# Forgetting attention with scores computed once by rows and probabilities transposed on TensorE, and a bias table stored from another queue

## The chip, the cores and the metric

The kernel runs on one core of a Trainium2 chip. The metric is device time in microseconds of one execution; the figure for the kernel before is the median of 3 runs. Engines: TensorE (PE in the rows; PEld is its weight load), VectorE (DVE), ScalarE (ACT), GpSimd (POOL) and SyncE (SP, whose queue is SPq).

## The reference, cut to what matters

One block of a hybrid encoder over 2048 tokens and 16 meta tokens, width 1024: input LayerNorm, one projection, two groups of 8 attention heads of size 64, output projection, mixture of experts. The change is in the second head group, forgetting attention, and in the store of a small table in the projection.

```python
def forgetting_attention(q, k, v, log_f, key_valid):
    ...
    cum = jnp.swapaxes(jnp.cumsum(log_f, axis=1), 1, 2)
    idx = jnp.arange(lp)
    for i in range(lp // Q_BLOCK):
        lo, hi = i * Q_BLOCK, (i + 1) * Q_BLOCK
        s = jnp.einsum('bqhd,bkhd->bhqk', q[:, lo:hi], k[:, :hi]).astype(jnp.float32) * (HEAD_DIM ** -0.5)
        s = s + cum[:, :, lo:hi, None] - cum[:, :, None, :hi]
        mask = (idx[None, :hi] <= idx[lo:hi, None]) & key_valid[None, :hi]
        p = jax.nn.softmax(jnp.where(mask, s, -jnp.inf), axis=-1)
        outs.append(jnp.einsum('bhqk,bkhd->bqhd', p.astype(v.dtype), v[:, :hi]))
```

The term of the query in `cum` drops out of the softmax; what is added to a score is the negated cumulative sum of its key (`ncum`).

## The kernel before, in words

Stages run one after another with a barrier between: projection (`phase_project`), window attention (`phase_window`), forgetting attention (`phase_forget`), output projection, routing, experts, combination. Everything is fp32. Where a product is to be exact, an operand x is split: ScalarE rounds it to a high part of type fp32r, VectorE computes the low part x - high, and the product is made of two or three fp32r matmuls.

**Forgetting attention** has 8 heads. A unit is one head and a group g = 0 to 3 of 512 queries (4 tiles j of 128), so 32 units. Keys are counted with the 16 meta keys first.

*Rows.* For each query tile (128 queries on partitions) the scores against all its keys are computed in chunks of up to 512 keys (`scores`, L1525): 5, 9, 13 and 17 chunks for the four groups, 44 a head, with 17,664 columns in all. Each chunk takes two matmuls (L1538, L1539), and the diagonal one a third that adds the mask (L1542). VectorE adds `ncum` and takes the maximum in one pass, writing in place in the PSUM bank (`maxima`, L1449, L1459); only the maximum is used. There are three such banks. `tops` (L1463) reduces them to the four negated maxima, splits these, and TensorE turns them to a row (`turn_tops`, L1546), which ScalarE copies into the extra partitions of `q_low` (`copy_tops`, L1383).

*Blocks.* The scores are computed a second time, transposed: for 128 keys on partitions against the unit's 512 queries (`block_scores`, L1554), 44 blocks and 17,664 columns a head, with two matmuls each (L1562, L1565; the second adds the turned maxima) and a mask (L1569). ScalarE takes the exponential twice from PSUM, once to fp32 (`p`, L1395) and once to fp32r (`p_hi`, L1396); VectorE makes `p_lo` (L1479). Four blocks later (`LAG`) `values` (L1573) multiplies by the values with three matmuls (L1582 to L1584); a column of ones among the values gives the sum of the probabilities. At a unit's end ScalarE copies the result (L1402), TensorE turns it back (L1590), and VectorE divides (`divide`, L1482, L1489).

*Order.* `steps` (L1253) is a list written out by hand that all engines follow: beside the blocks of unit n stand the row chunks of unit n+1, spread over 0.66 of the unit, then its tops; beside groups 1 and 2 stand the splits of the next head's keys, queries and values. Each engine takes its share of each step in this order and cannot pass a wait.

**Projection.** It goes through the tokens in groups of 512 (`sb`), and for each through 13 chunks of 128 output columns (24 matmuls of 512 columns each, L621 to L623), with two PSUM banks. ScalarE copies a chunk out (`chunk_copy`, L409, L413) to one of three slots, and GpSimd's queue stores it (`store_chunk`, L327, L335), as it does h and v. In `sb == 0`, after chunk 2, the same queue stores the table of relative biases, 8 rows repeated to 128 partitions' worth each (L356); window attention reads it later.

## Time and profile before

| | us |
|---|---|
| median of 3 runs | 2567.87 (2563.67 to 2568.36) |
| the profiled execution | 2572.01 |
| its span, first to last instruction | 2570.4 |

| busy, over the span | us | share |
|---|---|---|
| PE | 2255.2 | 88% |
| PEld | 1802.4 | 70% |
| DVE | 1700.1 | 66% |
| ACT | 1556.4 | 61% |
| POOL | 349.2 | 14% |

Forgetting attention lies in some 590 of the 2570 us. The mean granted TensorE clock is 0.936 of the full 2.4 GHz. A row of a timeline gives start and duration in us; a duration is longer than the distance to the next instruction of the engine, because instructions overlap, so costs are best read from start to start. A stretch of time is counted from the span's start.

### The profile page before, as it was taken

What the parts mean: (1) busy time and instruction counts of PE and PEld (TensorE: products, weight loads), DVE (VectorE), ACT (ScalarE), POOL (GpSimd) and SP (SyncE); (2) the same over time, 40 slices, a digit from 0 to 9 for tenths busy, and PEclk for the clock granted to TensorE, in tenths of its full rate; (3) what the DMA queues carried; (4) which work ended last, traced back from release to release, by engine and by line L of the source; (5) the groups of instructions that cost most, each with busy time, mean ns of one, the idle gap of its engine ahead of it and who ended that gap; (6) DMA issues with size and microseconds to landing.
All of it is one profiled execution on the core that took longest, in us unless ns stands there. A gap on an engine that the chain in (4) does not pass through costs nothing. (4 is left out here: it accounts for less than half of the span.)

```text
span 2570.4 us, 35701 instructions
## 1 busy us (share of the span) xinstructions
PE 2255.2 (88%) x11310; PEld 1802.4 (70%) x11310; DVE 1700.1 (66%) x3003; ACT 1556.4 (61%) x2368; POOL 349.2 (14%) x448
## 2 busy tenths in 40 slices
PE   6989999668869999999979995499999999999970
PEld 5778888544547777777758884387888888788860
DVE  5223231166547888888743333798999999899976
ACT  4222241166638888778753332287888888788866
POOL 0111111100010000000000000122222222121211
PEclk9989999878969999999989997699999999999995
DMA  5544352242242222211033331599879778998837
GB/s 196 146 134 146 114 185 74 88 115 83 61 123 64 65 67 66 67 44 29 9 130 130 148 131 74 180 363 321 291 220 307 249 254 289 324 318 285 277 95 278
DMA packets 210017, 420.12 MB, mean 163 GB/s; under 512 B 36536, under 2 KB 86024, under 8 KB 209000
## 3 DMA queue, kind: packets, MB, share of 16 engines
q1 hardware_dynamic: 177368, 314.21, 35.8%
q0 software_dynamic: 32544, 104.58, 14.5%
q8 instruction: 57, 0.93, 0.1%
q14 instruction: 48, 0.39, 0.0%
HBM read 437.19 MB, written 86.39 MB: 204 GB/s over the span
## 5 line engine op out<-in xcount | busy, mean ns | idle before, releaser
L2420 DVE TENSOR_TENSOR moe_w_lo<-fetch_w_raw,moe_w_hi 128x1024 fp32r<-128x1024 f32 x376 | 435.6, 1219 | 12.5 <-ACT moe_w_hi L2349 12.4
L2349 ACT ACTIVATE moe_w_hi<-fetch_w_raw 128x1024 fp32r<-128x1024 f32 x376 | 369.1, 1054 | 79.4 <-DMA fetch_w_raw<-in_w_e_up_dram 39.4
L2474 PE MATMUL moe_ps_gu<-moe_w_hi,moe_xT_hi 128*128 128x512 f32 x736 | 293.3, 399 | 4.5 <-DVE moe_xT_lo L2431 4.5
L2476 PE MATMUL moe_ps_gu<-moe_w_hi,moe_xT_lo 128*128 128x512 f32 x736 | 289.4, 393 | 0.0
L2475 PE MATMUL moe_ps_gu<-moe_w_lo,moe_xT_hi 128*128 128x512 f32 x736 | 288.9, 392 | 0.0
L1395 ACT ACTIVATE fox_p<-fox_ps_t,fox_ncumT 128x512 f32<-128x512 f32 (+4 forms) x352 | 209.6, 596 | 118.2 <-PE fox_ps_t L1569 60.6
L1479 DVE TENSOR_TENSOR fox_p_lo<-fox_p,fox_p_hi 128x512 fp32r<-128x512 f32 (+4 forms) x352 | 199.6, 572 | 55.0 <-ACT fox_p_hi L1396 54.4
L1459 DVE CUSTOM_DVE_ANT_0 fox_ps_r<-fox_ps_r,fox_ncum 128x512 f32<-128x512 f32 (+4 forms) x352 | 198.2, 593 | 47.0 <-PE fox_ps_r L1539 25.9
L2426 DVE TENSOR_TENSOR moe_d_lo<-fetch_d_raw,moe_d_hi 128x1024 fp32r<-128x1024 f32 x184 | 213.1, 1220 | 10.7 <-ACT moe_d_hi L2357 8.4
L1396 ACT ACTIVATE fox_p_hi<-fox_ps_t,fox_ncumT 128x512 fp32r<-128x512 f32 (+4 forms) x352 | 207.8, 590 | 0.0
L413 ACT ACTIVATE proj_qk_out<-proj_ps_chunk 128x512 f32<-128x512 f32 x52 | 31.0, 598 | 269.8 <-PE proj_ps_chunk L623 254.6
L2357 ACT ACTIVATE moe_d_hi<-fetch_d_raw 128x1024 fp32r<-128x1024 f32 x184 | 179.5, 1058 | 0.0
L498 DVE TENSOR_TENSOR proj_w_lo<-proj_w_raw,proj_w_hi 128x2048 fp32r<-128x2048 f32 (+1 forms) x28 | 59.9, 2140 | 169.3 <-ACT proj_w_hi L405 169.3
L621 PE MATMUL proj_ps_chunk<-proj_hT_hi,proj_w_hi 128*128 128x512 f32 x416 | 165.4, 398 | 6.1 <-ACT proj_qk_out L413 5.7
L623 PE MATMUL proj_ps_chunk<-proj_hT_hi,proj_w_lo 128*128 128x512 f32 x416 | 163.7, 394 | 0.0
L622 PE MATMUL proj_ps_chunk<-proj_hT_lo,proj_w_hi 128*128 128x512 f32 x416 | 163.6, 393 | 0.0
L2474 PEld LDWEIGHTS moe_ps_gu<-moe_w_hi,moe_xT_hi 128*128 128x128 f32 x736 | 139.7, 190 | 33.7 <-DVE moe_xT_lo L2431 3.5
L2476 PEld LDWEIGHTS moe_ps_gu<-moe_w_hi,moe_xT_lo 128*128 128x128 f32 x736 | 139.5, 189 | 30.2
L2475 PEld LDWEIGHTS moe_ps_gu<-moe_w_lo,moe_xT_hi 128*128 128x128 f32 x736 | 139.6, 190 | 28.1
L2487 PE MATMUL moe_ps_y<-moe_d_hi,moe_hT_hi 128*128 128x512 f32 x368 | 148.3, 403 | 3.6 <-DVE moe_d_lo L2426 3.6
L2489 PE MATMUL moe_ps_y<-moe_d_hi,moe_hT_lo 128*128 128x512 f32 x368 | 145.2, 394 | 0.0
L2488 PE MATMUL moe_ps_y<-moe_d_lo,moe_hT_hi 128*128 128x512 f32 x368 | 144.8, 393 | 0.0
(327 smaller groups left out, 5284.2 us busy)
## 6 DMA issues: line engine op xcount, KB each, us to landing
fetch_w_raw<-in_w_e_gate_dram SPq DMA_DIRECT2D x192, 512.0 KB
fetch_w_raw<-in_w_e_up_dram SPq DMA_DIRECT2D x192, 512.0 KB
fetch_d_raw<-in_w_e_down_dram SPq DMA_DIRECT2D x92, 1024.0 KB
proj_w_raw<-in_w_in_dram SPq DMA_DIRECT2D x24, 1024.0 KB, 5.2
proj_xt<-in_x_dram SPq DMA_DIRECT2D x16, 512.0 KB
h<-proj_hrow POOLq DMA_DIRECT2D x16, 512.0 KB, 3.4
win_q_raw<-qT SPq DMA_DIRECT2D x32, 256.0 KB, 4.1
mix_o<-o SPq DMA_DIRECT2D x16, 512.0 KB, 4.4
```

The source lines that it names most:

```text
L621: nc.tensor.matmul(out, whi[:, k], hT_hi[:, k, cols], start=k == 0, stop=False)
L1395: nc.scalar.activation(p[0:keys, slot, 0:width], bank[0:keys, 0:width], ACT.Exp, bias=bias)
L1396: nc.scalar.activation(p_hi[0:keys, slot, 0:width], bank[0:keys, 0:width], ACT.Exp, bias=bias).then_inc(probs, 1)
L1459: nc.vector.tensor_tensor_reduce(out=bank, in0=bank, in1=ncum[:, h % 2, key:key + width], scale=1.0, scalar=10 * MASK, op0=ALU.add, op1=AL ...
L1479: nc.vector.tensor_tensor(p_lo[0:keys, slot, 0:width], p[0:keys, slot, 0:width], p_hi[0:keys, slot, 0:width].bitcast(F32), ALU.subtract).t ...
L2349: nc.scalar.activation(w_hi[:, k], w_raw[:, k].rearrange("p j n -> p (j n)"), ACT.Copy).then_inc(gu_high, 1)
L2357: nc.scalar.activation(d_hi[:, k], d_raw[:, k], ACT.Copy).then_inc(dn_high, 1)
L2420: nc.vector.tensor_tensor(w_lo[:, k], w_raw[:, k].rearrange("p j n -> p (j n)"), w_hi[:, k].bitcast(F32), ALU.subtract).then_inc(gu_split, 1)
L2426: nc.vector.tensor_tensor(d_lo[:, k], d_raw[:, k], d_hi[:, k].bitcast(F32), ALU.subtract).then_inc(dn_split, 1)
L2474: nc.tensor.matmul(out, xT_hi[:, slot, k], w_hi[:, k, cols], start=k == 0, stop=False)
L2475: nc.tensor.matmul(out, xT_hi[:, slot, k], w_lo[:, k, cols], start=False, stop=False)
L2476: done = nc.tensor.matmul(out, xT_lo[:, slot, k], w_hi[:, k, cols], start=False, stop=k == KT - 1)
```

## The change

- Scores are computed once, by rows. VectorE's pass over a chunk writes score plus `ncum` to an SBUF tensor `s` (two of them, by the group's parity) instead of in place. ScalarE takes the exponential in place there, once for each query tile (or two pieces where a tile has more than 1,040 keys), 24 pieces a head, with the negated maximum as bias and the sum as a second output.
- The probabilities are transposed by TensorE in 128 x 128 parts, up to 4 for a block, fp32, 152 a head. Blocks are now the 16 meta keys and then 128 keys each, 44 a head with 19,456 columns. TensorE does this for two blocks at a time, at each odd block, followed by the value products of two earlier blocks. ScalarE copies the turned block out of PSUM (high part), VectorE makes the low part from PSUM.
- Values: high and low part of the values stand side by side in one weight of 128 columns, so two matmuls a block. The turn back is an fp32 matmul with a matrix that adds the two halves.
- Row banks 2 instead of 3, banks for turned blocks 4 instead of 3. Row chunks are spread over 0.75 of a unit. Splits of keys and queries come in 4 pieces each, of values in 2; a key split is once 128 partitions rather than twice.
- The table of biases is stored from ScalarE's queue in `sb == 1` after chunk 5, instead of from GpSimd's in `sb == 0` after chunk 2.

```diff
@@ phase_project, gpsimd @@
                         store_v(META_N)
-                        pool.wait_ge(table_done, 1)
-                        pool.dma_start(t["table"][:, :, 0:BIAS_TAB],
-                                       table[:].unsqueeze(1).to_broadcast([A_HEADS, P, BIAS_TAB])).then_inc(table_stored, 16)
@@ phase_project, scalar @@
+                    if sb == 1 and i == 5:
+                        act.wait_ge(table_done, 1)
+                        act.dma_start(t["table"][:, :, 0:BIAS_TAB],
+                                      table[:].unsqueeze(1).to_broadcast([A_HEADS, P, BIAS_TAB])).then_inc(table_stored, 16)
@@ phase_forget @@
-        R_BANKS, T_BANKS = 3, 3
+        R_BANKS, T_BANKS = 2, 4
...
+        def steps():
+            SPREAD = 0.75
...
+                    rate = SPREAD / len(ahead)
+                    events += [(rate * (i + 0.5), "scores", r) for i, r in enumerate(ahead)]
+                    for j in range(4):
+                        done = sum(len(row_chunks(4 * g + i)) for i in range(j + 1))
+                        events.append((rate * (done + 0.4), "tops", 4 * (n + 1) + j))
+                        mine = [r for r in range(pieces_before[n + 1], pieces_before[n + 2]) if pieces[r][1] == j]
+                        events += [(rate * (done + 0.8) + 0.14 * SPREAD * (i + 0.5) / len(mine), "exp", r)
+                                   for i, r in enumerate(mine)]
...
+            def exponential(r):
+                n, j, c, key, width = pieces[r]
+                g = units[n][1]
+                act.wait_ge(maxed, 4 * n + j + 1)
+                wait(act, summed, n - GROUPS4 + 1)
+                at = row_at[g][j] + key
+                here = s[g % 2][:, at:at + width]
+                nc.scalar.activation(here, here, ACT.Exp, bias=ntop[:, n % 2, j:j + 1],
+                                     accum_out=part[g][:, j, c:c + 1]).then_inc(probs, 1)
+
+            def probabilities_high(k):
+                n, b, keys, skip = blocks[k]
+                act.wait_ge(p_turned, k + 1)
+                wait(act, pv_done, k + 1 - P_SLOTS)
+                nc.scalar.activation(p_hi[0:keys, k % P_SLOTS, skip:SBT], ps_t[k % T_BANKS][0:keys, skip:SBT], ACT.Copy
+                                     ).then_inc(p_high, 1)
...
+                nc.vector.tensor_tensor_reduce(out=s[g % 2][:, at:at + width], in0=ps_r[r % R_BANKS][:, 0:width],
+                                               in1=ncum[:, h % 2, key:key + width], scale=1.0, scalar=10 * MASK,
+                                               op0=ALU.add, op1=ALU.max, accum_out=mx[g][:, j, c:c + 1]).then_inc(biased, 1)
...
+                wait(pe, biased, r - R_BANKS + 1)
...
+                nc.tensor.matmul(out, q_two[:, u, queries], k_hi[:, u, keys], start=True, stop=False)
+                done = nc.tensor.matmul(out, q_two[:, u, queries], k_lo[:, u, keys], start=False, stop=not last)
...
+            def turn(k):
+                n, b, keys, skip = blocks[k]
+                g = units[n][1]
+                wait(pe, p_split, k + 1 - T_BANKS)
+                out = ps_t[k % T_BANKS]
+                for j in range(skip // P, 4):
+                    if b == TILES:
+                        pe.wait_ge(probs, pieces_before[n] + sum(len(row_pieces(4 * g + i)) for i in range(j + 1)))
+                    at = row_at[g][j] + (0 if b == TILES else META + b * P)
+                    done = nc.tensor.transpose(out[0:keys, j * P:(j + 1) * P], s[g % 2][:, at:at + keys], ident[:])
+                done.then_inc(p_turned, 1)
...
+                nc.tensor.matmul(out, v_two[0:keys, u, b], p_hi[0:keys, slot, skip:SBT], start=b == TILES, stop=False)
+                nc.tensor.matmul(out, v_two[0:keys, u, b], p_lo[0:keys, slot, skip:SBT], start=False, stop=b == 4 * g + 3
+                                 ).then_inc(pv_done, 1)
...
+                    done = nc.tensor.matmul(ps_o[n % 2][:, j * P:j * P + HD], oT[:, n % 2, j * P:(j + 1) * P], pair_sum[:],
+                                            start=True, stop=True)
...
+            for what, which in steps():
                 if what == "block":
-                    block_scores(which)
-                    if which >= LAG:
-                        values(which - LAG)
...
+                    if which % 2 == 1:
+                        turn(which - 1)
+                        turn(which)
+                        for k in (which - 1 - LAG, which - LAG):
+                            if k >= 0:
+                                values(k)
+                    if which in back_at:
+                        turn_back(back_at[which])
```

## Rows read from the trace of the kernel before

**Rows 1.** Stretches: us, busy PE, PEld, DVE, ACT, POOL (instructions), PEclk, DMA share, GB/s
```profile
735.00:1322.00 587.00, 547.11 (x2994) 416.14 (x2994) 452.72 (x1240) 451.38 (x820) 34.90 (x38) 0.97 0.21 53
120.00:125.00 5.00, 4.26 (x10) 3.40 (x11) 0.00 (x0) 0.91 (x2) 0.54 (x1) 0.51 0.60 225
640.00:650.00 10.00, 8.83 (x51) 5.34 (x49) 6.93 (x26) 7.24 (x25) 1.04 (x2) 1.00 0.40 110
```

**Rows 2.** Waits of 745 to 1313 us: who for whom, total us, times, longest
```profile
ACT fox_p L1395 <- PE fox_ps_t L1569: 60.4, 73, 4.2
...
DVE fox_p_lo L1479 <- ACT fox_p_hi L1396: 54.1, 97, 1.8
```

**Rows 3.** Timeline, 1302 to 1304 us: start, duration, engine, line, operation
```profile
1302.63 0.39 PE L1562 MATMUL fox_ps_t<-fox_q_two,fox_k_two 128*128 128x512 f32 x1
...
1302.72 0.68 ACT L1396 ACTIVATE fox_p_hi<-fox_ps_t,fox_ncumT 128x512 fp32r<-128x512 f32 x1
...
1303.29 0.69 ACT L1395 ACTIVATE fox_p<-fox_ps_t,fox_ncumT 128x512 f32<-128x512 f32 x1
...
1303.78 0.39 PE L1562 MATMUL fox_ps_t<-fox_q_two,fox_k_two 128*128 128x512 f32 x1
```

**Rows 4.** Lines 1395 and 1489: duration ns min/median/max, first and last start, forms
```profile
L1395 ACT ACTIVATE fox_p<-fox_ps_t,fox_ncumT x352: 246/688/720, 745.1 to 1313.1; 128x512 f32<-128x512 f32 x112, 128x272 f32<-128x272 f32 x16, 16x16 f32<-16x16 f32 x16, 128x400 f32<-128x400 f32 x16
...
L1489 DVE TENSOR_TENSOR fox_o<-fox_ps_o,fox_inv x32: 424/424/425, 767.7 to 1316.7; 128x256 f32<-128x256 f32 x32
```

**Rows 5.** Timeline, 1012 to 1016 us, inside forgetting attention
```profile
1012.42 0.23 PE L1582 MATMUL fox_ps_o<-fox_p_hi,fox_v_hi 128*65 128x144 f32 x1
...
1012.49 0.23 PE L1583 MATMUL fox_ps_o<-fox_p_hi,fox_v_lo 128*64 128x144 f32 x1
...
1013.06 0.69 DVE L1479 TENSOR_TENSOR fox_p_lo<-fox_p,fox_p_hi 128x512 fp32r<-128x512 f32 x1 [0.67 <-ACT fox_p_hi L1396]
...
1013.67 0.44 DVE L1459 CUSTOM_DVE_ANT_0 fox_ps_r<-fox_ps_r,fox_ncum 128x272 f32<-128x272 f32 x1
...
1014.03 0.14 DVE L1459 DVE_READ_ACCUMULATOR2_ANT fox_mx<- 128x1 f32 x1
...
1015.20 0.61 ACT L1402 ACTIVATE fox_oT<-fox_ps_o 65x512 f32<-65x512 f32 x1
...
1015.68 0.71 ACT L1395 ACTIVATE fox_p<-fox_ps_t,fox_ncumT 128x512 f32<-128x512 f32 x1
```

**Rows 6.** Timeline, 1905.5 to 1907 us: eight fp32 transposes in the experts' stage
```profile
1905.92 1.04 PE L2496 MATMUL moe_ps_x<-ident,moe_x 128*128 128x128 f32 x8
...
1906.71 0.47 PE L2487 MATMUL moe_ps_y<-moe_d_hi,moe_hT_hi 128*128 128x512 f32 x1
```

**Rows 7.** Timeline, 659 to 661 us, in window attention
```profile
659.69 0.42 DVE L951 CUSTOM_DVE_ANT_0 win_s<-win_ps_s,win_bias,win_sink 128x208 f32<-128x208 f32 x1
659.78 0.46 ACT L872 ACTIVATE win_s<-win_s,win_ntop 128x208 f32<-128x208 f32 x1
...
660.03 1.04 PE L1067 MATMUL win_ps_o<-win_pT,win_v_prev 80*64 80x512 f32 x2 [0.36 <-DVE win_pT L965]
660.04 0.08 DVE L951 DVE_READ_ACCUMULATOR2_ANT win_top<- 128x1 f32 x1
...
660.23 0.46 ACT L872 ACTIVATE win_s<-win_s,win_ntop 128x208 f32<-128x208 f32 x1
...
660.91 0.59 PE L1068 MATMUL win_ps_o<-win_pT,win_v_cur 128*64 128x512 f32 x1
```

**Rows 8.** The table's store (KB, us to landing), and waits of 85 to 135 us
```profile
table<-proj_table POOLq DMA_DIRECT2D x1, 1280.0 KB, 32.2
...
ACT proj_qk_out L413 <- DMA qT<-proj_qk_out: 15.2, 1, 15.2
...
PE proj_ps_chunk L621 <- ACT proj_qk_out L413: 4.7, 1, 4.7
...
PE proj_ps_chunk L614 <- ACT proj_qk_out L413: 2.3, 1, 2.3
```

419 lines of the change are left out of this document (140 added, 279 removed).

## The prediction

> **What bounds the kernel now.** I read the busy times by stage first. The forgetting-attention stage fills most of 735 to 1322 us; in it TensorE is busy 547.11 of 587.00 us at a granted clock of 0.97, VectorE 452.72, ScalarE 451.38 [rows 1]. Busy TensorE time is modelled, so I looked next at who waits: ScalarE waits 60.4 us for one kind of TensorE product alone, VectorE 54.1 us for ScalarE [rows 2]. The timeline confirms it: a full 512-column block takes five matmuls and the next block's first starts 1.15 us after this one's (1302.63 to 1303.78), 0.23 us each with no gap; ScalarE's second exponential is followed after 0.57 us (1302.72 to 1303.29) [rows 3]. So TensorE sets the rate, and the two others are close behind. The 32 results of this stage come from 767.7 to 1316.7 us, 549.0 us for 31 units, 17.71 each, 70.8 us a head [rows 4]. In the first stage there is one accident of queueing: the bias table's store takes 32.2 us to land, a ScalarE copy waits 15.2 us for a store, and TensorE waits 4.7 and 2.3 us for ScalarE [rows 8], with a clock of 0.51 right after [rows 1].
>
> **Prices.** All from start to start, since durations overlap. Matmul: 0.23 us at 512 columns [rows 3], 0.07 at 144 (1012.42 to 1012.49) [rows 5]: 0.435 ns a column plus 0.007 us. VectorE: 0.61 at 512 (1013.06 to 1013.67), 0.36 at 272 (1013.67 to 1014.03) [rows 5]: 1.04 ns plus 0.08 us. ScalarE's copy out of PSUM: 0.48 at 512 (1015.20 to 1015.68) [rows 5], which I take as 0.94 ns a column; its exponential 0.57 [rows 3], as 0.84 ns plus 0.14 us. An exponential that also sums: 0.45 at 208 columns (659.78 to 660.23) [rows 7], 0.13 over that line. fp32 transpose of 128 columns: eight in 0.79 us (1905.92 to 1906.71) [rows 6], 0.099 each.
>
> **TensorE, per head.** Row scores stay: 44 chunks, 2 matmuls each and 16 masks, 37,376 columns, 17.0 us. Before, block scores add 37,376 columns in 108 matmuls, 17.0; values 52,992 in 132, 24.0; turning maxima and results some 2.3. Sum 60.3, against 70.8 measured: 10.5 a head for changes of operand shape and for waits. After, block scores and turned maxima go. Added are 152 transposes at 0.099, 15.0, and for 22 pairs about 0.08 each to start, 1.8. Values are 2 matmuls over 19,456 columns (a separate 16-key block of 512 columns in every unit makes that more than 17,664), 17.5. The turn back becomes 16 fp32 matmuls of 64 columns; the fp32 one of 512 columns is two records and takes 0.88 us (660.03 to 660.91) [rows 7], so 0.11 us by columns, twice that at most with two weight loads; I take 0.2, 3.2. Sum 54.5.
>
> **VectorE, per head.** Maxima before and after: 17,664 columns, 44 operations, 21.9. Low parts before 21.9, after 19,456 columns, 23.7. Small maxima 2.4 to 3.0, division 2.2 to 3.0, splits 6.0 to 6.2. Sum 54.4 before, 57.8 after. The maxima now write to SBUF rather than in place in PSUM. The trace of before has that form in window attention: 0.35 at 208 columns (659.69 to 660.04) [rows 7], where my line gives 0.30; so between 0 and 0.06 more an operation, 0 to 2.6 us. I take 0: the line is from the same operation at more like its widths.
>
> **ScalarE, per head.** Before: 88 exponentials over 35,328 columns 42.0, copies and splits 11.6, sum 53.6. After: copies of turned blocks 18.3; exponentials once, 17,664 columns in 24 pieces, 18.2 and 3.1 to 5.5 for sums; the rest 7.5. Sum about 48. It is off the path except at a unit's end.
>
> **Which is late, unit by unit.** A unit's blocks run beside the next unit's rows, so VectorE's load for the four periods of a head is 8.0, 15.4, 21.5 and 12.9 us, TensorE's 7.5, 12.5, 18 and 16.5 (the last has 62 transposes and only 5 row chunks). The larger ones sum to 61.4. VectorE becomes the bound in three periods. On top come hops. Transposes are issued for pairs, at the odd block, so ScalarE's copy of the even block waits there, and so does every exponential queued behind it; VectorE's low part of the even block is asked for at the same step as the transposes; and with two row banks instead of three TensorE is at most two chunks ahead, while a pair's turn and values hold it 0.87 plus 0.92 us. VectorE has about two maxima and one low part, 1.6 us, to cover that. I bound the wait per pair between 0.1 (full cover) and 0.7 us (neither the copy nor the next row is covered), and take 0.35: 22 pairs, 7.7. So 69.1 a head instead of 70.8, 535.5 for 31 units: **-13**.
>
> **Start of the stage.** The first probability now starts at 745.1 [rows 4], behind the transposed sums, the first maxima turned, and two-thousand-column splits. After, five row chunks, four exponentials and eight splits of some 0.5 us stand before the first block; about 738: **-7** (0 to -10, as the loads are the same).
>
> **The table store.** It leaves GpSimd's queue, where stores of the projection stood behind it, and is issued from ScalarE at the second group of tokens, after its sixth chunk. Lost were 4.7 and 2.3 us of waits [rows 8] and about 4 from the lower clock after them: **-11**. What may stay: the same 1280 KB move, and ScalarE is held while it issues; behind it is the copy of the next chunk, some 5.5 us later by 24 matmuls of 0.23, with two banks, so up to 8 us are hidden. Bounds -13 to 0. That ScalarE waits for a store and not for PSUM [rows 8] shows the delay as one of order within GpSimd's queue. The Trainium skill says otherwise of the move (DMA: Bandwidth & Descriptors, Issuing engines are not separate DMA queues): the DMAs of all issuing engines run on the same 16 DMA engines and interleave. By that the table would disturb as before and the -11 would be 0; no row shows this store from another queue.
>
> **Sum.** The profiled execution took 2572.01 us, 1.6 more than its span of 2570.4, and 4.1 more than the median of 2567.87. 2572.0 - 13 - 7 - 11 = 2541; against the median, 2537.
>
> **Rivals.** (A) The pair lockstep costs 0.62 us a pair. For it: two row banks, and an engine queue that can't pass a wait; against it: rows interleave with blocks. 0.27 more in 176 pairs is +48: 2585, slower. It decides from 0.35 + 31/176 = 0.53 us a pair. (B) The engines cover each other, 0.12 a pair: -40, 2497. For it: the queues run far enough ahead today that TensorE has no gap in [rows 3]; against: three engines within 15% of each other leave little slack. (C) The change of queue doesn't do what it says: the table's 1280 KB delay weights and stores in the second group as they did in the first. The rest as forecast: 2548. (D) TensorE, less dense and with transposes, falls to its 1.2 GHz level for parts of the stage. At it each product takes twice as long: 54.5 more a head, of which the 14.6 us of slack under 69.1 take up a part and 40 are left. A fifth of the stage so is 8 x 40 x 0.2 = +64: 2601. Against it: in window attention, between 640 and 650 us, the clock was 1.00 with TensorE busy 8.83 of 10 us on a mix with transposes [rows 1]. The Trainium skill would have it worse (TensorE: Matmul & The Clock Gate, Part 4: PE-mode transpose): transposes don't count as busy in the same way and the full clock doesn't engage for them. A stretch of that mix at 1.00 contradicts it so far as it goes.
>
> **How the numbers follow.** Forecast 0.42 (2537, itself good for 2518 to 2556), A 0.19, B 0.15, C 0.15, D 0.09. The range leaves out D, the upper part of A and the lower part of B: 2496 to 2588. A measurement of this kernel tells about 0.2%, 5 us, from no change. Faster by that: nearly all of the forecast, B, most of C: 0.69. Within: the mild end of A and the upper end of C, 0.08. Slower: 0.23.
>
> **What would show it.** The results' times should be 69 us a head (62 to 78 for the rivals); VectorE's busy time in the stage should rise from some 450 to about 470 us, ScalarE's fall below 410, while TensorE's matmul records thin out. VectorE's longest waits should be for the copies of turned blocks and for row scores, not small; if TensorE's clock in the stage is below 0.9, D holds. Transposes 0.099 us apart, low parts out of PSUM 0.61. First probability block before 740 us. In the first stage no wait of ScalarE for a qT store, and window attention starting some 11 us earlier. The forecast is wrong if TensorE stands without a gap after the change as before it, or if an exponential of 1,040 columns on ScalarE regularly holds up both others.

## The result and the profile after

The changed kernel takes 2620.12 us (median, 2615.49 to 2621.4) against 2568.11 us (2563.67 to 2569.42) before: a ratio of 1.0208, 95% interval 1.0192 to 1.0225. It is 2% slower. The forecast was 2537, the range 2496 to 2588, so both the sign and the range were wrong. The profiled execution of after took 2621.1 us, 2.1 more than its span of 2619.0.

Where the 48.6 us between the spans (2570.4 and 2619.0) arose is read off four marks: three starts of an instruction, and the end. Forgetting attention begins, by VectorE's first instruction there, at 719.35 us before and 714.23 after: -5.1. From there to the first result it took 48.4 us before [rows 4] and 50.5 after: +2.1. From the first to the last result it took 549.0 us before [rows 4] and 602.9 after: +53.9. From the last result to the end it took 1253.7 and 1251.4 us: -2.3. All of the loss is in the steady part of forgetting attention. The small terms are no larger than what single executions differ by: in the nine changed kernels of this document that are the same up to forgetting attention, it begins between 709.6 and 715.4 us.

The lines of after that answer to [rows 4] (results, and the first ScalarE product of a block):

```profile
L1421 DVE TENSOR_TENSOR fox_o<-fox_ps_o,fox_inv x32: 423/425/425, 764.7 to 1367.6; 128x256 f32<-128x256 f32 x32
...
L1341 ACT ACTIVATE fox_p_hi<-fox_ps_t x352: 258/591/602, 738.5 to 1363.8; 128x512 fp32r<-128x512 f32 x112, 16x512 fp32r<-16x512 f32 x16, 128x384 fp32r<-128x384 f32 x16, 128x128 fp32r<-128x128 f32 x16
```

The stretches of after, in the columns of [rows 1]. The first is the stage, the second a piece of it:

```profile
735.00:1372.00 637.00, 537.31 (x2992) 430.69 (x2992) 455.36 (x1337) 391.80 (x832) 24.07 (x32) 0.92 0.19 47
...
1100.00:1120.00 20.00, 19.49 (x77) 15.21 (x77) 13.36 (x37) 11.23 (x21) 0.75 (x1) 0.67 0.03 7
```

No engine has more work than foretold: VectorE is busy 455.36 us, ScalarE 391.80, in a stretch that is 50 us longer than that of [rows 1]. TensorE was busy 93% of the stretch before and is busy 84% of it now, and part of that at the lower of its two levels (granted clock 0.67 between 1100 and 1120). The time has gone into waiting, so the next view is who waits for whom (735 to 1366 us; total us, times, longest):

```profile
ACT fox_p_hi L1341 <- PE fox_ps_t L1474: 221.7, 150, 4.4
PEld fox_ps_r L1458 <- DVE fox_mx L1395: 116.2, 129, 5.0
PE fox_ps_r L1458 <- DVE fox_mx L1395: 76.0, 65, 4.6
DVE fox_k_lo L1372 <- ACT fox_k_hi L1315: 41.2, 21, 3.7
DVE fox_q_two L1376 <- ACT fox_q_two L1320: 40.1, 25, 2.2
DVE fox_p_lo L1408 <- ACT fox_p_hi L1341: 29.4, 70, 2.0
DVE fox_s L1395 <- PE fox_ps_r L1459: 29.0, 47, 1.7
...
DVE fox_v_two L1380 <- ACT fox_v_two L1325: 16.8, 7, 2.4
```

The three engines wait in a ring. ScalarE waits 221.7 us for transposes of probabilities, TensorE 76.0 us for VectorE's maxima (the row PE; the row PEld is the weight load of the same product), and VectorE 41.2 + 40.1 + 16.8 = 98.1 us for the high parts of the next head's keys, queries and values, which ScalarE makes, 53 times. That third wait is hardly there in the kernel before. Its two rows there, from the same view of 735 to 1320 us:

```profile
DVE fox_k_two L1437 <- ACT fox_k_two L1370: 3.3, 1, 3.3
DVE fox_q_low L1442 <- ACT fox_q_two L1376: 1.0, 1, 1.0
```

One turn of the ring stands in the timeline of after, 841 to 852 us (start, duration, engine, line; in square brackets the idle time before it and what ended it):

```profile
841.79 0.60 ACT L1341 ACTIVATE fox_p_hi<-fox_ps_t 128x512 fp32r<-128x512 f32 x1 [0.33 <-PE fox_ps_t L1474]
842.29 0.62 ACT L1320 ACTIVATE fox_q_two<-fox_q_raw 128x512 fp32r<-128x512 f32 x1
...
842.94 0.69 DVE L1376 TENSOR_TENSOR fox_q_two<-fox_q_raw,fox_q_two 64x512 fp32r<-64x512 f32 x1 [1.65 <-ACT fox_q_two L1320]
...
846.00 0.93 ACT L1334 ACTIVATE fox_s<-fox_s,fox_ntop 128x768 f32<-128x768 f32 x1 [1.78 <-DVE fox_ntop L1403]
...
847.19 0.94 ACT L1334 ACTIVATE fox_s<-fox_s,fox_ntop 128x784 f32<-128x784 f32 x1
...
848.12 0.67 ACT L1325 ACTIVATE fox_v_two<-fox_v_raw 128x576 fp32r<-128x576 f32 x1
...
848.83 0.76 DVE L1380 TENSOR_TENSOR fox_v_two<-fox_v_raw,fox_v_two 128x576 fp32r<-128x576 f32 x1 [2.40 <-ACT fox_v_two L1325]
...
849.84 0.68 DVE L1395 CUSTOM_DVE_ANT_0 fox_s<-fox_ps_r,fox_ncum 128x512 f32<-128x512 f32 x1
...
850.58 0.79 PE L1458 MATMUL fox_ps_r<-fox_k_hi,fox_q_two 128*128 128x512 f32 x1 [4.52 <-DVE fox_mx L1395]
```

ScalarE's copy of a turned block waits 0.33 us for TensorE after an exponential (841.79), and its high part of the queries is behind that copy (842.29). VectorE, whose low part stands at the same step, has done its earlier work and stands 1.65 us. A few us later ScalarE has two exponentials of 0.93 us ahead of the values' high part (846.00, 847.19, then 848.12); VectorE stands 2.40 us at the low part, with row scores ready in both banks and their maxima queued behind the wait; TensorE, with both banks full, stands 4.52 us. The next matmul is at half the clock (0.79 us where full speed gives 0.39; the granted clock is 0.65 from 850.5 to 855). This is no single accident: TensorE stands 4.51 to 4.59 us for a maximum seven times, once beside each head that has a next one, each time with matmuls of some 0.8 us right behind it, and 2.50 us another seven times, some 11 us later. These 14 stops are 49 of its 76.0 us. ScalarE's own wait of 1.78 us before the first exponential is for VectorE's maxima of the tile, which closes the ring.

### The profile page after: what moved, and what is told of

Same layout as the page of the kernel before. It is cut to its first block and busy times, and to the rows that moved or that the text cites. A ratio compares the mean times of both kernels' runs of the same rounds, so it can differ in the third digit from the quotient of the medians.

```text
span 2619.0 us, 35938 instructions
## 1 busy us (share of the span) xinstructions
PE 2237.8 (85%) x11293; PEld 1810.8 (69%) x11293; DVE 1706.7 (65%) x3112; ACT 1500.0 (57%) x2389; POOL 332.1 (13%) x435
## 5 line engine op out<-in xcount | busy, mean ns | idle before, releaser
L2317 DVE TENSOR_TENSOR moe_w_lo<-fetch_w_raw,moe_w_hi 128x1024 fp32r<-128x1024 f32 x376 | 435.5, 1218 | 12.9 <-ACT moe_w_hi L2246 12.6
L1341 ACT ACTIVATE fox_p_hi<-fox_ps_t 128x512 fp32r<-128x512 f32 (+4 forms) x352 | 180.7, 532 | 222.8 <-PE fox_ps_t L1474 221.7
L1458 PE MATMUL fox_ps_r<-fox_k_hi,fox_q_two 128*128 128x512 f32 (+4 forms) x352 | 150.0, 426 | 97.7 <-DVE fox_mx L1395 76.0
L1408 DVE TENSOR_TENSOR fox_p_lo<-fox_ps_t,fox_p_hi 128x512 fp32r<-128x512 f32 (+4 forms) x352 | 210.2, 612 | 32.1 <-ACT fox_p_hi L1341 29.4
L1395 DVE CUSTOM_DVE_ANT_0 fox_s<-fox_ps_r,fox_ncum 128x512 f32<-128x512 f32 (+4 forms) x352 | 193.7, 569 | 35.9 <-PE fox_ps_r L1459 29.0
L1474 PE MATMUL fox_ps_t<-ident,fox_s 128*128 128x128 f32 (+1 forms) x1216 | 182.1, 290 | 19.5 <-ACT fox_s L1334 18.5
L1334 ACT ACTIVATE fox_s<-fox_s,fox_ntop 128x144 f32<-128x144 f32 (+5 forms) x192 | 173.2, 903 | 19.0 <-DVE fox_ntop L1403 18.9
L1474 PEld LDWEIGHTS fox_ps_t<-ident,fox_s 128*128 128x128 f32 (+1 forms) x1216 | 145.6, 144 | 45.6 <-ACT fox_s L1334 23.1
L1458 PEld LDWEIGHTS fox_ps_r<-fox_k_hi,fox_q_two 128*128 128x128 f32 x352 | 72.0, 205 | 149.1 <-DVE fox_mx L1395 116.6
```

The costliest lines, as they stand in the source:

```text
L1341: nc.scalar.activation(p_hi[0:keys, k % P_SLOTS, skip:SBT], ps_t[k % T_BANKS][0:keys, skip:SBT], ACT.Copy).then_inc(p_high, 1)
L1395: nc.vector.tensor_tensor_reduce(out=s[g % 2][:, at:at + width], in0=ps_r[r % R_BANKS][:, 0:width], in1=ncum[:, h % 2, key:key + width], s ...
L1408: nc.vector.tensor_tensor(p_lo[0:keys, k % P_SLOTS, skip:SBT], ps_t[k % T_BANKS][0:keys, skip:SBT], p_hi[0:keys, k % P_SLOTS, skip:SBT].bi ...
L1458: nc.tensor.matmul(out, q_two[:, u, queries], k_hi[:, u, keys], start=True, stop=False)
L1474: done = nc.tensor.transpose(out[0:keys, j * P:(j + 1) * P], s[g % 2][:, at:at + keys], ident[:])
L2317: nc.vector.tensor_tensor(w_lo[:, k], w_raw[:, k].rearrange("p j n -> p (j n)"), w_hi[:, k].bitcast(F32), ALU.subtract).then_inc(gu_split, 1)
```

## The experiments

All times below are medians. The kernel before, on the same chips, gave 2564.2 us beside the first four, 2567.75 beside the next four and 2567.15 beside the last four; the ratios are against it. The last column is from the one profiled execution of each kernel. It can be off by some 7 us: nothing in the stage differs between e1 and e7, nor between e5 and e11, and it gives 535.9 and 529.1 for the one pair, 493.4 twice for the other.

| kernel | us | ratio (95%) | first to last result, us |
|---|---|---|---|
| after | 2620.12 | 1.0208 (1.0192 to 1.0225) | 602.9 |
| e1_lag: low splits two blocks later | 2539.93 | 0.9905 (0.9888 to 0.9923) | 535.9 |
| e2_single: block by block | 2536.46 | 0.9901 (0.9882 to 0.992) | 527.5 |
| e3_before_table: kernel before, table's store moved | 2561.87 | 0.9995 (0.9981 to 1.0008) | 550.2 |
| e4_before_nolag: kernel before, low splits at once | 2616.54 | 1.0207 (1.019 to 1.0224) | 597.9 |
| e5_lag_single: e1 and e2 | 2500.3 | 0.975 (0.9728 to 0.9773) | 493.4 |
| e6_lag_single_r3: e5, 3 row banks | 2505.24 | 0.9762 (0.9742 to 0.9782) | 498.6 |
| e7_lag_spread: e1, store in 8 pieces | 2534.38 | 0.9884 (0.9866 to 0.9903) | 529.1 |
| e8_lag1: low splits one block later | 2575.73 | 1.0041 (1.0025 to 1.0057) | 566.3 |
| e9_lag_turn1: e1, transposes singly | 2517.4 | 0.9804 (0.9788 to 0.9821) | 511.4 |
| e10_lag_val1: e1, values singly | 2520.36 | 0.982 (0.98 to 0.9838) | 510.8 |
| e11_all: e5, store in 8 pieces | 2492.55 | 0.9712 (0.969 to 0.9733) | 493.4 |
| e12_gpsimd_splits: e2, low splits by GpSimd | 2478.31 | 0.9654 (0.9638 to 0.967) | 474.1 |

Two theories stood at the start. One: VectorE loses its lead because its low splits stand at the very step of ScalarE's high splits; in the kernel before they stood one or two parts later. Two: the pair order itself locks the engines (rival A), wherever the splits are. The differences below are between medians; made from the ratios, which take out what the chips differ by, they shift by up to 4 us.

### The splits later (e1_lag)

The changed kernel with one edit on VectorE's side of the list; the computation is the same.

```diff
             for what, which in steps():
                 if what == "block":
+                    last_block = which
...
+                    while late and late[0][0] <= which:
+                        split_low(*late.pop(0)[1])
...
                 elif what == "split":
-                    split_low(*which)
+                    if which[0] == 0:
+                        split_low(*which)
+                    else:
+                        late.append((last_block + 2, which))
```

> The changed kernel with one edit: VectorE makes the low part of each key, query or value split two blocks after ScalarE's high part instead of at the same step. Theory S (VectorE stands at a split until ScalarE, queued behind exponentials and pair copies, has rounded it; 98 us of such waits in the stage after the change): the waits for L1315, L1320 and L1325 fall below 20 us, a head goes from 80.2 to about 70 us, the first to the last result from 602.9 to about 540 us, and the time to about 2560. Theory P (the pair order holds the engines in lockstep, 0.8 us a pair, whatever the splits do): VectorE's wait moves to low parts and row scores, a head stays at 77 or more, time 2595 or more.

Measured 2539.93 us: 80 us less than after, 24 less than before. From 735 to 1300 us no wait for a split is left among VectorE's waits, and TensorE's wait for maxima has fallen from 76.0 to 28.2:

```profile
ACT fox_p_hi L1341 <- PE fox_ps_t L1481: 164.6, 146, 6.1
...
PE fox_ps_r L1465 <- DVE fox_mx L1395: 28.2, 55, 0.8
```

The longest wait for a maximum is 0.8 us: the stops of 4.5 and 2.5 us are gone. The stage's clock is back at 0.97. First to last result is 535.9 us. The mean time between the results of a head, over seven heads, falls from 24.2, 19.9, 23.4 and 12.5 us in after to 16.2, 18.3, 23.4 and 12.6. The gain stands in the two periods that hold splits and nowhere else. So the splits' place is a cause, and taking it away is enough to undo the whole loss. The case named for the pair order alone (2595 or more) has not come, and the gain is 20 us larger than the case named for the splits (2560). That the splits' place is the only cause does not follow.

### Block by block (e2_single)

The splits stay at their old step; only TensorE's order is changed.

```diff
-                    if which % 2 == 1:
-                        turn(which - 1)
-                        turn(which)
-                        for k in (which - 1 - LAG, which - LAG):
-                            if k >= 0:
-                                values(k)
+                    turn(which)
+                    if which >= LAG:
+                        values(which - LAG)
```

> The changed kernel with one edit: TensorE transposes and multiplies block by block at every step, not by pairs at odd ones. Theory P: ScalarE's copy of the even block no longer waits, -5 us a head or more, time below 2580. Theory S: the stall at the splits stays, at most -2 us a head, time 2600 to 2625.

Measured 2536.46 us, 84 less than after. The direct waits for splits shrink but stay, 18.1 + 16.8 + 10.3 = 45.2 us. VectorE's, 735 to 1300 us:

```profile
DVE fox_s L1395 <- PE fox_ps_r L1459: 21.9, 38, 0.8
DVE fox_q_two L1376 <- ACT fox_q_two L1320: 18.1, 18, 2.2
DVE fox_v_two L1380 <- ACT fox_v_two L1325: 16.8, 7, 2.4
...
DVE fox_k_lo L1372 <- ACT fox_k_hi L1315: 10.3, 14, 1.1
```

The values' wait is the same as in after, 16.8 us in seven times, up to 2.4. What it costs TensorE is not: its longest wait for a maximum is 1.1 us here (22.2 us in all), 4.6 there. So the pair order also makes the same stop of VectorE dearer.

Either edit alone removes the whole loss. The case named here for the splits alone (2600 to 2625) has not come, as that for the pairs alone had not in e1. How much belongs to each, these two runs cannot tell: it takes both edits together.

### The move of the table's store alone (e3_before_table)

The kernel before, with this part of the change only.

```diff
-                        pool.wait_ge(table_done, 1)
-                        pool.dma_start(t["table"][:, :, 0:BIAS_TAB],
...
+                    if sb == 1 and i == 5:
+                        act.wait_ge(table_done, 1)
+                        act.dma_start(t["table"][:, :, 0:BIAS_TAB],
```

> The kernel before with the table store alone moved to ScalarE's queue, as the change does. The prediction had -11 us; the trace after shows window attention starting 3.2 us earlier and new waits for stores and a load beside the store. Theory M (the same 1280 KB disturb another place): -2 to -5 us, 2563 to 2566. Theory Q (a matter of GpSimd's queue alone): -10 us or more, 2558 or less.

Measured 2561.87 against 2564.2 us; the interval of the ratio, 0.9981 to 1.0008, includes 1. That allows the smaller gain named for theory M or none at all, and excludes the 10 us or more of theory Q. The wait is moved, not removed. From 85 to 135 us TensorE is now busy all 50.00 us; from 250 to 300, where the store has gone, it is busy 42.51. Waits there:

```profile
ACT proj_junk L376 <- DMA proj_xt<-in_x_dram: 12.2, 1, 12.2
...
PE proj_ps_chunk L622 <- ACT proj_qk_out L410: 7.5, 1, 7.5
```

A load of tokens is late in place of a store of queries. The forecast's ground for -11 was that the delay is one of order within GpSimd's queue; that is refuted, since from another queue and in the next group of tokens the same volume delays another queue's load. Rival C is right. The Trainium skill (DMA: Bandwidth & Descriptors, Issuing engines are not separate DMA queues) says that DMAs of all issuing engines interleave on the same DMA engines; this trace agrees, with 42.94 us of 50 busy before at 85 to 135 and 42.51 of 50 now at 250 to 300.

### The old kernel with its splits at once (e4_before_nolag)

The reverse test: the kernel before, its low parts moved up to the step of the high ones.

```diff
                 elif what == "split":
-                    split_low(*which)
+                    part = {0: 2, 2: 3, 4: 5, 5: 6, 6: 7}.get(which[1])
+                    if part:
+                        split_low(which[0], part)
```

> The kernel before with one edit: VectorE makes the low part of a split at the step at which ScalarE makes the high part (before: one or two steps later). Theory S: VectorE waits for ScalarE at 35 splits of 1 to 3 us; VectorE has 16 us of slack a head here, so a part is hidden: +5 to +25 us, waits for ScalarE's splits above 30 us. Theory P: no change, within 3 us.

Measured 2616.54 us, 52 more, twice the most that was expected (+25): the slack of VectorE did not hide a part. The splits' place alone costs the old kernel, which turns no pairs, as much as the whole change cost. Yet VectorE's direct waits for splits here are small, from the waits of 735 to 1365 us:

```profile
DVE fox_ps_r L1459 <- PE fox_ps_r L1541: 46.3, 50, 2.8
...
DVE fox_k_two L1437 <- ACT fox_k_two L1370: 11.3, 8, 3.3
DVE fox_q_low L1442 <- ACT fox_q_two L1376: 6.6, 8, 1.0
```

17.9 us stand for a loss of 49 between the results. The rest is knock-on: TensorE waits 40.6 us for the maxima's split parts (22.6 before), among them one wait of 3.3 to 3.4 us beside each of seven heads (1.3 at most before), and VectorE 46.3 for row scores (25.8 before). What a stop costs is not its own length; an engine that stops lets the other two run dry. A part of it may go through the clock: the stage's is 0.95 instead of 0.97, and TensorE is busy 568.05 us (735 to 1365) instead of 547.11 with the same work. How the remaining 31 us divide among these is not shown. A low split of 1,536 columns also takes VectorE 1.76 us here and stands at another place than before, which the run doesn't separate from the meeting itself.

### Both edits (e5_lag_single)

> The changed kernel with both edits: VectorE's low splits two blocks after ScalarE's high splits, and each block turned and multiplied at its own step. One cause (the meeting of ScalarE and VectorE at the splits, which pairs only feed): the two edits repair the same wait, each alone already took it away, and both together give 2530 to 2540 us, at most 5 better than the better of them, some 69 us a head. Two causes that add (splits 80 us and pairs 80 us of separate loss): would give below 2500 us and 62 us a head, which is the sum of the larger loads alone.

Measured 2500.3 us, below the case named for one cause (2530 to 2540) and at the edge of the one named for two (below 2500). First to last result is 493.4 us, 64 to 65 a head. So, in us:

| | low splits at once | two blocks later |
|---|---|---|
| pairs | 2620 | 2540 |
| block by block | 2536 | 2500 |

By the ratios times 2568 us, the pair order costs 79 us beside immediate splits and 40 beside later ones; the splits' place costs 78 with pairs and 39 without. Two causes, then, each with its own loss of some 40 us, and 39 more when they meet. Why they meet is how I read it, and not shown by a run of its own: pairs make ScalarE late for the split that VectorE waits for (the direct waits for keys and queries are 81.3 us with pairs and 28.4 without), and they make TensorE stand longer for the same stop (4.6 us against 1.1, above). The expectation that one cause was being mended twice was wrong. The stage in this kernel (735 to 1250 us), and the longest wait of ScalarE, VectorE or TensorE there:

```profile
735.00:1250.00 515.00, 484.97 (x2978) 387.26 (x2976) 450.32 (x1329) 397.71 (x827) 23.76 (x32) 1.00 0.22 56
```

```profile
ACT fox_p_hi L1341 <- PE fox_ps_t L1481: 66.4, 144, 2.0
```

ScalarE's wait for transposes shows what the pairs did: 221.7 us in after, 164.6 with later splits, 66.4 here.

### Row banks (e6_lag_single_r3)

```diff
-        R_BANKS, T_BANKS = 2, 4
+        R_BANKS, T_BANKS = 3, 3
```

> As the one with both edits, but three PSUM banks for row scores and three for turned blocks instead of two and four. If the two row banks bound how far TensorE runs ahead of VectorE's maxima, the wait of TensorE for maxima (22 to 30 us in the two single edits) goes and the time falls by 10 to 20 us, to about 2520. If VectorE's and TensorE's work is what remains, the time stays within 5 us of the one with both edits.

Measured 2505.24 us, 5 more than with two and four; the intervals of the two ratios overlap. TensorE's weight loads wait less for maxima, 18.7 us against 41.7, but its wait for the low part that frees a bank of turned blocks grows from 2.2 us to 20.6:

```profile
PEld fox_ps_t L1481 <- DVE fox_p_lo L1408: 20.6, 36, 1.0
PEld fox_ps_r L1465 <- DVE fox_mx L1395: 18.7, 37, 0.8
```

So a third row bank, paid for with one of the turned blocks', gains nothing here. Both kinds of bank are freed by VectorE, and a bank given to one is taken from the other. With pairs, where I had named the two row banks as a ground of rival A, no run changes them.

### How late is late enough (e8_lag1)

e1 with `last_block + 1` in place of `last_block + 2`.

> The changed kernel, pairs kept, with VectorE's low split one block after ScalarE's high split instead of two. In pair order two consecutive blocks are one step of TensorE, so ScalarE runs up to a pair late. If what costs is that VectorE asks for the split before ScalarE can have passed its wait for the pair's transposes, one block of distance removes it for about half of the splits: 2560 to 2590 us, with VectorE waiting 30 to 60 us for ScalarE's splits. If any distance does because VectorE's own low part of a block already waits for ScalarE ahead of it, 2535 to 2545 us.

Measured 2575.73 us: one block of distance gives 44 of the 80 us, two give all. The waits for splits are down to 9.3, 7.5 and 5.2 us (98.1 in after), yet 36 us of loss are left; again the knock-on outweighs the waits themselves. The time is in the first case named; the waits, 22.0 us in all, are below the 30 to 60 named with it. ScalarE can be a pair behind in pair order, so one block of distance was to catch about half of the splits: 21 waits are left of 53.

### Which half of the pair (e9_lag_turn1, e10_lag_val1)

Both carry the later splits of e1. One issues each block's transposes at its own step and keeps values in pairs, the other does the opposite.

```diff
+                    turn(which)
                     if which % 2 == 1:
-                        turn(which - 1)
-                        turn(which)
                         for k in (which - 1 - LAG, which - LAG):
```

> The changed kernel with the low splits two blocks later, and of the pair order only the half that holds ScalarE taken away: each block's four transposes are issued at its own step, the values still two blocks at a time at the odd one. With whole pairs this is 2540 us, block by block 2500 us. If the 40 us between them come from ScalarE held at the even block (its copy of turned blocks waits 165 us for transposes, 146 times, in the pair order, 66 us block by block), this gives 2500 to 2510 us. If they come from TensorE's lump of four products of values, which lets no row scores through to VectorE, it stays at 2530 to 2540 us.

> The opposite half: low splits two blocks later, transposes still for two blocks at the odd step, values one block at each step. If ScalarE held at the even block is the cause, this stays at 2530 to 2545 us, with ScalarE waiting some 150 us for transposes. If the lump of values is the cause, it gives 2500 to 2510 us. If each is half of it, both mixed kernels give about 2520 us.

Measured 2517.4 and 2520.36 us: 22.5 and 19.6 us less than e1, where both halves together give 40 (by the ratios 26 and 22). Neither half is the whole cause, each is about half of it, the last case that the second expectation names. Their waits differ as their mechanisms do. ScalarE's for transposes, first of e9, then of e10:

```profile
ACT fox_p_hi L1341 <- PE fox_ps_t L1481: 85.8, 121, 3.0
```

```profile
ACT fox_p_hi L1341 <- PE fox_ps_t L1481: 137.1, 144, 3.1
```

With transposes singly ScalarE is held little longer than in e5 (85.8 us against 66.4), with values singly much longer (137.1), and the time is nearly the same. So the hold on ScalarE is not the whole cause. What the two halves share is a lump on TensorE, 0.79 us for eight transposes and 0.92 for four values, during which VectorE gets no row scores; that this is the other part is argued, not shown.

### The table's store in pieces (e7_lag_spread, e11_all)

```diff
-                    if sb == 1 and i == 5:
-                        act.wait_ge(table_done, 1)
-                        act.dma_start(t["table"][:, :, 0:BIAS_TAB],
-                                      table[:].unsqueeze(1).to_broadcast([A_HEADS, P, BIAS_TAB])).then_inc(table_stored, 16)
+                    if sb >= 1 and i in (3, 6, 9):
+                        piece = 3 * (sb - 1) + i // 3 - 1
+                        if piece < 8:
+                            act.wait_ge(table_done, 1)
+                            act.dma_start(t["table"][:, 16 * piece:16 * piece + 16, 0:BIAS_TAB],
+                                          table[:].unsqueeze(1).to_broadcast([A_HEADS, 16, BIAS_TAB])
+                                          ).then_inc(table_stored, 16)
```

> The changed kernel with the low splits two blocks later (2539.9 us) and with the bias table's store cut into 8 pieces of 16 rows, 160 KB each, issued from ScalarE three to a group of tokens instead of 1280 KB at once. If the burst is what disturbs the first stage (waits of ScalarE for a qT store and for x, of TensorE for ScalarE, window attention at 504 instead of 496 us), the waits go and the time falls by 6 to 10 us to about 2532. If what disturbs it is the volume moved, or if nothing of the start of window attention hangs on it, it stays at 2540 within 3 us.

> The changed kernel with low splits two blocks later, blocks turned and multiplied one at a time, and the table's store in 8 pieces of 16 rows. If the two stages' gains are independent, the 5.5 us that the spread store gave beside the pair order stand again: 2494 to 2496 us, window attention starting at 493 us. If the spread moves traffic into something that only the pair order's slack hid, it stays at 2500 us.

Measured 2534.38 us beside e1's 2539.93, and 2492.55 beside e5's 2500.3. The intervals of the two ratios overlap a little in both pairs, so that the time fell by about 6 and 8 us (5 and 10 by the ratios) is likely rather than certain; that the waits are gone is plain. TensorE from 250 to 300 us in e7 is busy throughout, where in after it is busy 42.71 us:

```profile
250.00:300.00 50.00, 50.00 (x278) 43.15 (x277) 13.15 (x17) 11.75 (x17) 5.87 (x11) 1.00 0.36 125
```

No wait of TensorE for ScalarE is left there (7.3 us in after), and window attention, by its load of the bias table, begins at 493.0 us (494.1 in e11) instead of 503 to 506 in the kernels that store it from ScalarE at once. The 11 us that I had forecast for the change of queue come, at that place, from cutting the burst of 1280 KB. Not all of them stand in the medians; where the rest goes stays open.

### The low splits on GpSimd (e12_gpsimd_splits)

Block by block, splits at their old step, but made by an engine that has only the results' stores to do beside them.

```diff
-            for n, (h, g) in enumerate(units):
+            def split_low(h, what, i):
...
+                    pool.wait_ge(k_high, PIECES * h + i + 1)
+                    nc.gpsimd.tensor_tensor(k_lo[:, u, K_COLS[i]], k_raw[:, K_COLS[i]], k_hi[:, u, K_COLS[i]].bitcast(F32),
+                                            ALU.subtract).then_inc(k_split, 1)
...
+            for what, which in steps():
+                if what == "split":
+                    split_low(*which)
+                elif what == "block" and which - 3 in back_at:
+                    store(back_at[which - 3])
```

> The changed kernel with blocks turned and multiplied one at a time (2536 us with VectorE's low splits at the step of ScalarE's high ones), and all low splits of keys, queries and values made by GpSimd, which follows the same order and waits for nothing else but the outputs that it stores; each split there also waits for the one before. If the loss of that kernel against the 2500 us with later splits is VectorE standing at a split until ScalarE has made the high part, it goes here as well without any delay of the split: at most 2505 us. If, beyond that, VectorE's work bounds the stage (it is busy 468 of 493 us with both edits), the 6 us a head of splits come off it and the time falls below 2490, down to 2460. If GpSimd is slow at it (no row shows such an operation on it) or slows VectorE by its use of the same memory, TensorE waits for the splits at a head's start: 2510 to 2560 us.

Measured 2478.31 us, the fastest of all: 58 below e2, 22 below e5, 3.5% below the kernel before. The waits for high parts are still there, but it is GpSimd that has them, and nobody waits for it:

```profile
POOL fox_v_two L1317 <- ACT fox_v_two L1356: 142.1, 14, 18.4
...
POOL fox_q_two L1313 <- ACT fox_q_two L1351: 67.3, 28, 3.6
...
POOL fox_k_lo L1309 <- ACT fox_k_hi L1346: 56.0, 21, 3.7
```

TensorE's own waits in the stage (735 to 1235 us) are 21 us in all:

```profile
PE fox_ps_t L1486 <- ACT fox_s L1365: 18.5, 24, 1.3
PE fox_ps_r L1470 <- DVE fox_mx L1411: 2.2, 8, 0.4
```

and it is busy nearly throughout, 750 to 1230 us:

```profile
750.00:1230.00 480.00, 459.16 (x2914) 380.83 (x2912) 398.36 (x1221) 384.10 (x807) 111.99 (x100) 1.00 0.22 56
```

In this kernel TensorE sets the rate again, with a head in 61.9 us. That VectorE's 6 us a head less work were worth the step from e5 down (493.4 to 474.1 us between results, 2.5 a head) is the expectation's reading and fits: TensorE's weight loads wait 18.3 us for maxima, 41.7 in e5. But the expectation took VectorE as busy 468 of 493 us in e5, a number that includes the start of the next stage; in the stage itself it is 450.32 of 515.

## Why the prediction was wrong, point by point

**The pair's hop.** The sum for the steady part was 61.4 us a head of larger loads and 22 pairs at 0.35 us. With the splits later, and the pairs kept, the results take 535.9 us; the forecast for them was 535.5. The sum was right for that kernel, but not its two parts. Block by block with later splits (e5) a head takes 64.7 us (mean of seven), not 61.4; the pairs bring it to 70.4 (e1), 0.26 us a pair and not 0.35. Seven heads take 492.9 us where 483.7 was forecast, and the last three periods, beside which no next head is prepared, 43.0 where 51.8 was. These misses hide one another, and that is luck. So is that e1's whole time, 2539.93, is 3 us from the forecast, as the terms for the start and the table are not borne out below. The forecast described a kernel in which the splits cost only their work.

**The step that failed: the splits counted as work alone.** The working has "splits 6.0 to 6.2" in VectorE's list, and nothing on where they stand. The change moved VectorE's low parts from one or two parts behind ScalarE's high parts to the same step, and I costed that at nothing without naming a cover. Naming what is queued behind the wait finds it: behind VectorE's wait for a split stand the maxima that free TensorE's two row banks; ahead of ScalarE's split stand a copy that waits for a pair's transposes and exponentials of 0.93 us. It cost 80 us (after against e1) and in the old kernel 52 (e4). The forecast's own sign shows it too: VectorE's longest waits were to be for turned blocks and for row scores (29.4 and 29.0 us), and they are for the splits of keys and queries (41.2 and 40.1). In the terms of rival A after makes (80.0 - 61.4) / 22 = 0.85 us a pair, above the 0.7 that I had as the upper bound, because the bound was made from the pair's own products and from no other wait.

**Rival A** has the sign and part of the size: it gave 2585 and a cause of its own is there, 79 us beside immediate splits and 40 beside later ones. Its ground of in-order queues is borne out (e9, e10). Its ground of two row banks is open: a third gave nothing block by block (e6), and with pairs it was not run.

**The table, -11.** Wrong: nothing measurable (e3), as rival C had it. The row of the store [rows 8] showed that ScalarE waited for a store; it did not show whose place in which queue made it late, and I chose the reading by which the change helps. The answer of after to the bottom of [rows 8] has the same kind of wait at another place, from the waits of 250 to 300 us:

```profile
ACT proj_junk L376 <- DMA proj_xt<-in_x_dram: 11.9, 1, 11.9
...
PE proj_ps_chunk L622 <- ACT proj_qk_out L410: 7.3, 1, 7.3
...
ACT proj_qk_out L410 <- DMA qT<-proj_qk_out: 5.3, 1, 5.3
```

"No wait of ScalarE for a qT store" did not hold either. TensorE loses 7.3 us there, as much as the 4.7 and 2.3 of before.

**The start, -7.** The first block stands at 738.5, before 740 as foretold, against 745.1 [rows 4]. But 5 of these 6.6 us were there when the stage began, by VectorE's first instruction in it, in after and then in before:

```profile
714.23 0.23 DVE L1424 TENSOR_TENSOR fox_pair_sum<-ident 128x64 f32<-128x64 f32 x1 [6.79 <-PEq L92]
```

```profile
719.35 0.17 DVE L1493 MEMSET fox_mx<- 128x8 f32 x4 [6.76 <-PEq L92]
```

From there to the first block it is 25.8 us before and 24.3 after, to the first result 48.4 and 50.5. The mark I had given could not tell an earlier start of the stage from a shorter start-up; the term was near -1.5 at the block and gone by the result. Nor are the 5 us all of the change's making: e4, the same as before up to this stage, begins it at 716.6.

**The clock.** The stage's is 0.92, above the 0.9 that I had set for rival D, but 0.67 in a stretch of it. The transposes of this mix alone don't lower it: with the same 1,216 of them it is 0.97 with later splits, 1.00 in e5 (735 to 1250 us) and 1.00 from 750 to 1230 us in e12. In after the stops of 4.5 us each have matmuls at half speed right behind them. In e1, where no stop is that long, there are four other stretches at the lower level (granted clock 0.57 from 880 to 886 us, behind waits of at most 1.0 us from 871 on), so what else lowers it stays open. The clock is also a part of the price. For the same work TensorE is busy 537.31 us in after, 484.97 in e5 and, in e1:

```profile
735.00:1295.00 560.00, 508.67 (x2980) 406.64 (x2979) 453.35 (x1327) 389.97 (x830) 23.52 (x32) 0.97 0.21 52
```

So up to 29 of the 80 us between after and e1, and up to 24 of the 40 between e1 and e5, are products at the lower level. Rival D had the transposes as a reason, which these runs don't bear out, and has the lower clock as a cost, which they do. No run parts the stops from the clock behind them. The Trainium skill (TensorE: Matmul & The Clock Gate, Part 4: PE-mode transpose) says that the full clock doesn't engage for transposes; e12's stretch contradicts it for a mix of transposes and matmuls like this one.

**VectorE's busy time** was to rise from some 450 to about 470 us. It stayed: 452.72 before, 455.36 in after, 450.32 in e5. The low parts rose as foretold (199.6 to 210.2 us), but the maxima, which now write to SBUF, fell from 244.7 to 220.2 with their reads of the result (140 ns each before, 82 after). From start to start one of 512 columns takes 0.60 us (849.84 to 850.44 above), so the price of 0.61 held.

**What held.** ScalarE below 410 us (391.80). Transposes 0.099 us apart and the turn back 0.2 us a product: eight transposes of after take from 806.45 to 807.24 us, and a turn back, four products with two records each, from 808.25 to 809.09. Timeline of after:

```profile
806.45 1.04 PE L1474 MATMUL fox_ps_t<-ident,fox_s 128*128 128x128 f32 x8
807.24 0.48 PE L1485 MATMUL fox_ps_o<-fox_p_hi,fox_v_two 128*128 128x512 f32 x1
...
808.25 1.00 PE L1492 MATMUL fox_ps_o<-fox_pair_sum,fox_oT 128*128 128x64 f32 x8
809.09 1.04 PE L1474 MATMUL fox_ps_t<-ident,fox_s 128*128 128x128 f32 x8
```

These prices were right. TensorE's sum of 54.5 us a head may be low: e12 has it busy 459.16 of 480 us at 61.9 us a head, which is 59.2; since busy time is modelled and includes the overlap of one product's end with the next, this run can't say by how much.

## What to carry to other kernels

When two engines follow one list in order, and one makes what the other consumes, put the consumer some steps behind the producer, and cost a change that takes this distance away, even if no operation is added: here it was worth 80 us of 2620 beside the pairs, 39 without them, and 52 in the kernel before. Work out a wait's price from what is queued behind it on both engines, since a stop makes the neighbours run dry and here had matmuls at half speed behind it, and its knock-on was larger than the wait itself in two of these kernels (e4, e8). The burst of DMA moved to another queue delayed something else here; cut into pieces among the work, it delayed no matmul.

## What the runs showed of the hardware beyond what was expected

GpSimd makes a low part of 128 x 512 from two operands in SBUF in 1.29 us, where VectorE takes 0.69 (both from groups by line; GpSimd's spans are rough):

```profile
L1309 POOL TENSOR_TENSOR fox_k_lo<-fox_k_raw,fox_k_hi 128x512 fp32r<-128x512 f32 x24 | 30.9, 1289 | 31.3 <-ACT fox_k_hi L1346 30.9
```

VectorE's own operations were hardly slower beside it. Its low parts of 128 x 512 of the probabilities, in e5 and then in e12, 750 to 1220 us:

```profile
L1408 DVE TENSOR_TENSOR fox_p_lo<-fox_ps_t,fox_p_hi 128x512 fp32r<-128x512 f32 x203 | 136.9, 682 | 4.1 <-ACT fox_p_hi L1341 3.3
```

```profile
L1424 DVE TENSOR_TENSOR fox_p_lo<-fox_ps_t,fox_p_hi 128x512 fp32r<-128x512 f32 x216 | 147.1, 686 | 7.7 <-ACT fox_p_hi L1372 5.6
```

682 ns became 686. Of these and of the maxima of 512 columns, 118 overlap in time with one of GpSimd's low parts, and none of them takes more than 0.69 us. The Trainium skill (SBUF — State Buffer, SBUF: two separate sides) has VectorE and GpSimd exclude each other when VectorE's operation has two inputs in SBUF and GpSimd's reads SBUF (or when VectorE's runs in a two-port mode). VectorE's here have one of theirs in PSUM, and the trace agrees that they don't exclude each other then. No run here shows the case with both in SBUF.

One spread stays unexplained: from the last result to the end it was 1253.7 us before, 1251.4 in after and 1248.1 in e1, though nothing there was changed. It is of the size by which single executions differ ahead of the stage, too.
